# Mixer's residual copied back into the accumulating PSUM banks, three quarters of one down matrix loaded into hT and hg during the routing, first gates in finer pieces

## The reference, cut to what matters

```python
h = x
for layer in range(DEPTH):                      # 2 layers
    hn = rms_norm(h, attn_norm_g[layer])
    mix = mixer_ab(...) if layer % 2 == 0 else mixer_c(...)
    h = h + mix
    ff = hierarchical_moe(rms_norm(h, ffn_norm_g[layer]), w_group[layer], w_expert_router[layer],
                          w_gate[layer], w_up[layer], w_down[layer])
    h = h + ff
return rms_norm(h, final_norm_g)
...
# hierarchical_moe: top 1 of 4 groups, then top 2 of its 8 experts, for each of 256 tokens
h = silu(xb @ w_gate[e]) * (xb @ w_up[e])       # e of 32 experts: 1024 x 512, 1024 x 512
return h @ w_down[e]                            # 512 x 1024
```

## Time and profile before

| | |
|---|---|
| median of 3 runs | 1155.87 us (1154.61 to 1157.15) |
| the profiled execution's own time | 1154.69 us |
| its span | 1152.9 us |
| PE busy | 834.0 us (72%) |
| DVE, ACT, POOL busy | 154.1, 153.8, 67.1 us |
| moved by DMA | 438.08 MB, mean 380 GB/s |
| chain that ended last | DMA 45%, PE 43%, issue 6% |

### The profile page before, as it was taken

One profiled execution on the slowest core, in us unless ns is written; L12 is line 12 of the kernel. 1 busy time (PEld: TensorE's weight loads), 2 busy tenths in 40 slices (PEclk: granted clock), 3 DMA queues, 4 the chain that ended last, 5 costly groups with the idle time before them and its releaser, 6 DMA issues.

```text
span 1152.9 us, 13900 instructions
## 1 busy us (share of the span) xinstructions
PE 834.0 (72%) x5880; PEld 431.6 (37%) x5880; DVE 154.1 (13%) x420; ACT 153.8 (13%) x341; POOL 67.1 (6%) x86
## 2 busy tenths in 40 slices
PE   9999998666556564738799999966646564646597
PEld 8555783141313131303354576332313122222235
DVE  2142431000000000000014534100000000000002
ACT  2345241000000000000010444000000000000001
POOL 0010120000000000000001542000000000000000
PEclk9999999797978696969799999978878787887798
DMA  9942759999999999999999548999999999999993
GB/s 381 421 191 75 292 219 405 427 427 429 426 428 427 427 428 428 427 427 427 428 424 422 203 157 313 425 426 429 427 428 424 430 426 430 427 428 429 428 429 151
DMA packets 37089, 438.08 MB, mean 380 GB/s; under 512 B 4144, under 2 KB 5168, under 8 KB 10288
## 3 DMA queue, kind: packets, MB, share of 16 engines
q1 hardware_dynamic: 36464, 434.92, 90.0%
q10 hardware_dynamic: 576, 2.44, 0.5%
HBM read 436.30 MB, written 1.05 MB: 379 GB/s over the span
## 4 chain that ended last, share of the span: by engine, by line
DMA 45%; PE 43%; issue 6%; SPq 2%; DVE 2%; ACT 1%; POOL 0%; POOLq 0%; DVEq 0%; ACTq 0%
PE bank L1155 19%; DMA ring<-in_w_up 9%; PE bank L879 8%; DMA arena<-in_w_up 8%; DMA arena<-in_w_gate 8%; DMA ring<-in_w_down 7%; DMA ring<-in_w_gate 7%; DMA arena<-in_w_down 5%; PE bank L1025 5%; PE bank L915 2%; SPq L414 2%; PE bank L1296 1%; PE bank L858 1%; PE bank L1108 1%; DMA ring<-w_ab 1%
## 5 line engine op out<-in xcount | busy, mean ns | idle before, releaser
L1155 PE MATMUL bank<-ring,hg 128*32 128x512 f32 x1792 | 290.5, 707 | 267.0 <-DMA arena<-in_w_gate 72.9
L1155 PEld LDWEIGHTS bank<-ring,hg 128*32 128x32 f32 x1792 | 76.8, 127 | 453.6 <-issue 361.0
L1155 PE MATMUL bank<-arena,hg 128*32 128x512 f32 x256 | 140.5, 712 | 0.0
L1155 PE MATMUL bank<-ring,arena 128*32 128x512 f32 x704 | 107.0, 639 | 31.2 <-DMA ring<-in_w_down 18.4
L879 PE MATMUL bank<-ring,hg 128*128 128x512 f32 x224 | 98.9, 595 | 0.0
L1661 DVE TENSOR_TENSOR arena<-arena,bank 128x512 f32<-128x512 f32 x16 | 11.0, 688 | 539.2 <-PE bank L1155 539.2
L1025 PE MATMUL bank<-arena,ring 128*128 128x256 f32 x256 | 63.9, 388 | 0.0
L1155 PEld LDWEIGHTS bank<-ring,arena 128*32 128x32 f32 x704 | 28.9, 117 | 91.7 <-issue 77.2
L1155 PE MATMUL bank<-arena 128*32 128x512 f32 x192 | 59.8, 613 | 1.4 <-ACT arena L738 1.4
L879 PEld LDWEIGHTS bank<-ring,hg 128*128 128x128 f32 x224 | 41.7, 190 | 49.0 <-issue 48.5
L1108 PEld LDWEIGHTS bank<-arena,hr 128*128 128x128 f32 x448 | 51.1, 192 | 11.7 <-issue 11.7
(11 more groups left out here) (207 smaller groups left out, 657.2 us busy)
## 6 DMA issues: line engine op xcount, KB each, us to landing
ring<-in_w_up SPq DMA_DIRECT2D x56, 2048.0 KB, 21.6
ring<-in_w_gate SPq DMA_DIRECT2D x50, 2048.0 KB, 19.7
ring<-in_w_down SPq DMA_DIRECT2D x48, 2048.0 KB, 20.2
arena<-in_w_down SPq DMA_DIRECT2D x8, 2048.0 KB, 9.9
arena<-in_w_up SPq DMA_DIRECT2D x8, 2048.0 KB, 29.0
arena<-in_w_gate SPq DMA_DIRECT2D x8, 2048.0 KB, 27.9
ring<-w_ab SPq DMA_DIRECT2D x6, 2048.0 KB, 31.0
arena<-in_w_down SPq DMA_DIRECT2D x12, 1024.0 KB, 27.0
```

The costliest lines, as they stand in the source:

```text
L1155: op = pe.matmul(dst[rows, :], lhsT[:, q, rows], unit[s][:, q, cols], start=(q == 0), stop=(q == steps - 1))
```

## The change

1. One set of banks, 0 to 3 (`H_BANKS`), takes both mixers' output projections and both layers' experts. After DVE has added a chunk to `hT` it copies the chunk back into its bank (`h_put`; ACT does it for the eighth), so that `residual` is gone. What used those banks moves to banks 4 to 7: the retention, the logits, the turned rows, the turns in the windowed attention. `inner(0)` now waits for `cat` 4, and two of the turned rows wait for `ms_out` and for the first `hr_done`.
2. With `hT` no longer needed, and half of `hg` free after its rows are turned, three of the four rows of expert 3's down matrix per partition (1.5 of 2 MB) are loaded there, in two loads, as soon as the logits, the copies back and the low turned rows are through. `xeT` and `e_y` change places in `hg`.
3. The first gates go in parts of 1, 1, 2, 2 and 2 chunks, and `PIECES` has four pieces: an eighth, an eighth, a quarter, a half.
4. The fillers in the routing (3 and 2 matmuls) and between the last downs (3 times 4) are gone. In the last quad `combine`, `last_weights` and a filler of 24 matmuls come ahead of the gates. `copy_low` waits until both halves of the downs are done.
5. At the start the first chunk of x and weights is loaded alone. The first weights of the windowed attention are loaded in three pieces.
6. At the end the squares of three pairs of chunks are added on DVE before PE sums them, and the norm's factor is spread straight from `rstd` (no diagonal matrices).
7. In the windowed attention two pieces of the output projection move to after the next pair's scores.

```diff
-PIECES = [slice(0, 2 * DE), slice(2 * DE, 4 * DE), slice(4 * DE, UNIT)]
+PIECES = [slice(0, DE), slice(DE, 2 * DE), slice(2 * DE, 4 * DE), slice(4 * DE, UNIT)]
+EARLY_LOADS = 12
...
+        early_rows = [flat(hT[:])[:, 0:D], flat(hT[:])[:, D:2 * D], flat(e_y)]
...
+        FIRST_GATHERS = [((0,), 4), ((1,), 5), ((2, 3), 7), ((4, 5), 4), ((6, 7), 5)]
...
+                last_rows = expert_flat(l, QUAD - 1, 2)
+                sp.wait_ge(once["logits"], l + 1)
+                sp.wait_ge(h_put, KD * (l + 1))
+                sp.dma_start(flat(hT[:]), last_rows[:, 0:2 * D]).then_inc(m["low_landed"], 16)
+                sp.wait_ge(hr_turned, 4 * l + 2)
+                sp.dma_start(flat(e_y), last_rows[:, 2 * D:3 * D]).then_inc(m["low_landed"], 16)
                 for part, cols in enumerate(PIECES):
-                    if part < 2:
+                    if part < 3:
                         sp.wait_ge(m["low_used"], part + 1)
...
             def inner(pair):
                 if pair == 0:
                     pe.wait_ge(ab["rk"], 1)
+                    pe.wait_ge(ab["cat"], 4)
...
             def turn_rows(l, high):
                 pe.wait_ge(scaled, SCALED[2 * l + 1] + 4 * high + 4)
                 for b in range(NB):
+                    if high:
+                        pe.wait_ge((ms_out, hr_done)[b], (2 * l + 2, 4 * l + 1)[b])
...
                     if k >= 4:
-                        pe.wait_ge(h_done, KD * l + k - 3)
+                        pe.wait_ge(h_put, KD * l + k - 3)
...
-                stay_busy(3, ident, hg[:, 0, :])
...
-                stay_busy(2, ident, hg[:, 0, :])
...
                     gather_first(0)
+                    gather_first(1)
+                    gates(0, 1, "xe", 1).then_inc(m["low_used"], 1)
+                    gates(1, 2, "xe", 2).then_inc(m["low_used"], 1)
+                    gather_first(2)
+                    gather_first(3)
+                    gates(2, 4, "xe_high", 1).then_inc(m["low_used"], 1)
+                    gather_first(4)
+                    gates(4, 6, "xe", 3)
+                    gates(6, 8, "xe_high", 2).then_inc(m["used"], 1)
...
+                    if final:
+                        combine(i)
+                        last_weights()
+                        stay_busy(24, ident, ones[:])
...
-                    if second:
-                        residual()
...
                         for e in range(QUAD):
-                            if e:
-                                stay_busy(4, ident, last_y[:, 0, 0, :])
                             last_down(e, half)
...
             def mixer_out(l, done):
                 for k in range(KD):
                     dve.wait_ge(done, k + 1)
-                    residual(k, OUT_BANKS[l], bias=l == 1)
+                    residual(k, H_BANKS, bias=l == 1)
+                    if k < KD - 1:
+                        dve.wait_ge(h_done, KD * l + k + 1)
+                        dve.tensor_copy(chunk_of(H_BANKS, k), hT[:, k, :]).then_inc(h_put, 1)
```

More of the change, by code:

```diff
@@ L777, in experts @@
                 op.then_inc(m["pickT_sb"], 1)
+                silu(last)
                 copy_hidden(last)
@@ L1110, in gather, with gather_first @@
                         op.then_inc(m["gathered"], 1)
[L1112 to L1113 removed]
+                def gather_first(part):
+                    chunks, at = FIRST_GATHERS[part]
+                    if part == 0:
                         pe.wait_ge(m["pick"], 1)
[L1115 to L1116 removed]
+                        pe.wait_ge(hr_done, 4 * l + 4)
+                    for place, k in enumerate(chunks):
                         for b in range(NB):
[L1118 removed]
+                            op = pe.matmul(of_block(bank[at], place), hr[:, b, k, :], pick[:, b, :],
                                            start=(b == 0), stop=(b == NB - 1))
@@ L1154, in four @@
                             rows = slice(s * CAP, (s + 1) * CAP)
-                            op = pe.matmul(dst[rows, :], lhsT[:, q, rows], unit[s][:, q, cols],
+                            moving = unit[s][:, q, cols]
+                            if place == 0 and kind == 2 and s == QUAD - 1:
+                                moving = (*early_rows, unit[s][:, 0, :])[q][:, cols]
+                            op = pe.matmul(dst[rows, :], lhsT[:, q, rows], moving,
                                            start=(q == 0), stop=(q == steps - 1))
@@ L1164, in turn_weights @@
                     op.then_inc(m["pickT"], 1)
-                def residual():
-                    for k in range(KD):
-                        pe.matmul(chunk_of(Y_BANKS, k), ident, hT[:, k, :], start=k < 4, stop=False, skip_group_check=True)
                 def combine(i):
@@ L1247, in quad @@
                         pe.wait_ge(m["y_high"], i)
+                    if first:
+                        pe.wait_ge(once["rounds"], l + 1)
                     if not final:
@@ L1283, in _ @@
             experts(0)
-            pe.wait_ge(w_landed[AB_UNITS - RING + 0], 32)
-            chunks = [k for both in zip(ACT_CHUNKS, DVE_CHUNKS) for k in both]
             for b in range(NB):
-                for i, k in enumerate(chunks):
+                for i, k in enumerate(C_CHUNKS):
+                    for j, ks in enumerate(C_PIECES):
+                        if b == 0 and i == ks.start:
+                            pe.wait_ge((*first_in, w_landed[AB_UNITS - RING])[j], 32)
                     if b == 0 and i % 2 == 0:
```

225 lines of the change are left out of this document (115 added, 110 removed).

## The result

The changed kernel has a median of 1147.8 us (4 runs, 1146.78 to 1149.36) against 1155.8 for the one before (4 runs, 1154.61 to 1157.15): a ratio of 0.9931, interval 0.9917 to 0.9945. That is faster by 8.0 us, where 12.7 was forecast: inside the outer range of 1139 to 1150, outside the forecast's own range of 1140.5 to 1146.5. The profiled execution took 1146.78 with a span of 1145.0, 7.9 less than before.

What follows compares the result with a forecast made beforehand. Transfers were taken to bound the expert stages, PE the mixers and each stage's end. Terms -4.5 - 0.9 - 3.1 - 3.3 + 0.2 + 0.3 - 0.1 - 1.3 = -12.7 took 1155.87 to 1143.2 us; own range 1140.5 to 1146.5, outer 1139 to 1150.

Steps and rivals of the forecast that it cites:

- the early load buys nothing: Rival: small pieces run slowly or slots are not free in time, so both routing gains go; 1148.6 us, 15 in 100.
- layer 0's hole: Layer 0's routing: early down rows and an earlier first piece fill the stretch without transfers; -4.5 us.
- the start: First loads: PE starts earlier but the second piece holds three chunks and lands at about 8; +0.3 us, bounds 0 and +1.
- the end: Final sums: 32 matmul halves become 20 and two diagonals with their handover go; -1.3 us, bounds -1.6 and -0.8.
- the last quads: Last expert quads: work moved into the wait for gates leaves the end bound by last bytes; -3.1 (layer 1), -3.3 us (layer 0).
- the allowance for the clock: Layer 0's routing: PE's clock may fall as first gates begin, losing 1.5 us at six chances in ten; 0.9 taken off.
- 2, layer 1: Layer 1's routing: early rows close a 1.5 us loss, smaller pieces cost back about 0.6; -0.9 us, bounds -1.5 and 0.
- 4, edges: Mixer edges: `inner(0)` waits for a copy, +0.2 us; start +0.3; copies back with moved projection pieces -0.1.
- the second rival: Wait inside the last ups lowers the clock for long, so both layers lose 2.5 us; about 1154, 7 in 100.
- signs of being wrong: Second-quad traffic hole at 181 or later; clock 0.5 in first gates or last ups; layer 1 DVE period above 1; first unit ending after 21.
- signs of being right: No traffic gap from 162 to 190; first piece about 170.6; last quad at full clock, gates 7 us; final span 1.3 us shorter.
- the clock that stays low: Rival: half clock through the first gates' whole chain delays the last piece 11.5 us; about 1159 us, 5 in 100.

Runs made afterwards that it cites:

- the later one: Series that measured the changed kernel again, unedited: 1145.5 us (six runs), ratio 0.9912 to the kernel before.
- both orders tried apart: Changed kernel with the last quad's old order: 1152.31 us, 0.9973; kernel before with only its new order: 1150.66 us, 0.9952.
- the new order alone: Kernel before, with combination, last weights and 24 fillers ahead of the last gates, no fillers between downs: 1150.66 us, ratio 0.9952.
- the second execution: Second profiled execution of the changed kernel, unedited: span 1142.6 us; its series had a median of 1145.5 us, ratio 0.9912.
- the combined version: Changed kernel with start as before, three pieces, routing fillers of 3 and 2 matmuls, two fillers in the end's sums: 1143.50 us, 0.9895 to the kernel before.

## Why the prediction was right, and where it was off

The sign and the kinds of place held, the sum was 4.7 us too good in the first series and 2.0 in the later one, where the medians are 10.7 us apart (10.2 by the ratio). By the time alone, 1147.8 lies nearer to the rival "the early load buys nothing" (1148.6) than to the forecast; only the run without the early load tells them apart. The misses of the terms also cancel in part: in the first profiled execution layer 0's hole (+2.6), layer 1's (+0.7), the start (+1.3), `inner(0)` (+0.1) and the end (+1.2) fell short, the last quads (-0.5) and mixer 1 (-0.6) did better, 4.8 in all. By the terms, from the profiled executions:

- **1, layer 0's hole, -4.5.** The first execution had -1.9, the second -4.3. The mechanism was right, early load and issue time too: "about 170.6" is 8.95 us after the last unit, and 8.72 was measured at full clock. The term that was mis-sized is the allowance for the clock, 1.5 us "at six chances in ten, the 0.9". Half clock came in 13 of 16 routings and costs 2.5 us, since it reaches back before the gates: the last turned rows (1.01 instead of 0.66 us), the gathers (2.08 instead of 1.16) and the first gates (3.14 instead of 1.92) are all slower. At full clock 5.4 was priced and 4.3 came: the assumed 390 GB/s of the small pieces was 299 (176 to 180 us) and 338 (180 to 184) in the first execution, 296 (176 to 180) in the second.
- **2, layer 1, -0.9.** The last gates came 0.2 us sooner. The early load gave 1.0, but the four pieces cost most of it back (373 and 351 GB/s from 709 to 716); with three the gates came another 0.7 sooner.
- **3, last quads, -3.1 and -3.3.** -2.7 in layer 1 and -4.2 in layer 0 by the traces; both orders tried apart give 5.1 to 5.5 for the two. Right, and the largest term. One step in it was off: a half of the ups takes 7.06 us at full clock and not 6.1, so the first downs come at 28.8 instead of 27.9. The wait of 2.7 us in the ups did lower the clock in layer 1 (8.76 us for the half instead of 7.06), in the half that has the slack. In layer 0 the same program waited 2.64 us and kept it. In the new order alone it fell in the half without slack, in layer 0 (8.63 us), and the gain there was 2.3 instead of 4: the second rival's trigger, at a small price.
- **4, edges.** Mixer 1 gave -0.75 instead of -0.1; `inner(0)` +0.3 (0.2 said). The start cost +1.6 where +0.3 was said: the piece of three chunks "lands at about 8", but PE went on at 9.42 only (9.30 in the second execution), with 56 of 64 matmuls to do. The missing warm-up was not priced at all; with the old pieces two executions differ by 2 us, most likely by it.
- **5, the end, -1.3.** -0.1, and -0.8 and -1.6 in the second execution and the combined version. The 20 sums are one column wide and stand behind waits, and the clock fell in them. Where it held, as in the runs without the early load and without the 24 fillers, tails of 11.6 and 12.0 give -1.1 to -1.5: at full clock the term was right.

Of the signs of being wrong, three came in the first execution: a clock of 0.50 in the first gates, one of 0.57 in the last ups (1099.7 to 1103), and a first unit that ended at 21.8. Of the signs of being right, those on the last quad came; the stretch without a hole did not (53 GB/s from 174 to 176), nor the shorter tail. Of the rivals, the clock that stays low came in its small form: it turned no sign, as the bounds said (2.5 us, not 11.5). The Trainium skill, "TensorE: Matmul & The Clock Gate", Part 1, has the full clock as something that activity must earn. The routing bears that out: half clock in 13 of 16 routings without fillers and in one of 12 with them, at 2.5 us. The start goes the same way by its times (2 us, slow in nine of nine with six warm-ups and in one of five with seven), though the records of the clock read 1.00 there. At the end the change took out sums, not fillers; half clock cost about 1.5 us where it came, and no edit here is shown to prevent it. The Trainium skill, "DMA: Bandwidth & Descriptors", in the passage on the two cost components, adds a fixed cost to each load. The page measured it on loads that GpSimd issues, and these come from SP's queue. Here eight queued loads of 256 KB moved 2.1 MB at some 300 GB/s, 7 us and not the 21 that the prediction estimated by the page, so the fixed costs overlapped in the queue, and what is left is the slower rate of the small loads.

Open: the effect of the 24 fillers, why the clock holds in one execution of the same program and falls in another, whether a warm-up or a filler more would make start and end sure, and the waits of 0.3 to 1.7 us without a cause in the profile between matmuls of the last downs, which differ from kernel to kernel and stand in the kernel before too.

## What to carry to other kernels

A filler on PE can be part of the critical path's clock: price its removal like a stall, by the row of the next dependent matmuls at half clock, and size it to end just before the operand it waits for. The clock fell in some executions of a program and not in others, so several have to be profiled before a filler is called enough or useless. When a hole in the transfers is filled, ask what issues the next transfer, for that chain is the next limit. A piece's size trades an earlier issue against a slower transfer: by one execution each, four pieces won where the chain was the limit at full clock, three where the queue was full anyway.

## What was not expected of the hardware

The same program had the first piece at 11.05 and at 8.72 us in two executions, which differ there in the clock, with the waits of PE named in the timeline the same (0.79 and 0.78 us). Loads of 256 KB with 2 KB rows kept the DMA engines as busy (1.03) at 351 GB/s as loads of 512 KB with 4 KB rows at 407 (1.02). The first unit's 64 matmuls took 14.17 us in one execution with seven warm-ups, 16.08 in another with seven and 16.17 in one with six, with a granted clock of 1.00 in the records of that stretch each time.
